# Gated delta rule on one core: keys projected first, projection and scan joined in one block, the projection's last column written among the scan's first steps

## What is computed

```python
h = rms_norm(x) ;  q, k, v = silu(short_conv(h @ w_in))      # width-5 convolution along time
k, q = l2_norm(k), l2_norm(q) ;  g, beta = decays from h @ w_in
# chunks; L strictly lower, decay = exp(cum_i - cum_j)
T = (I + tril(k_beta @ k.T * decay, -1))^-1
state loop: v_new = u - w @ state ; o = (q e^g) @ state + (q k.T * decay) @ v_new ; state = ...
out = o_forward + flip(o_backward)
```

## Time and profile before

| what | value |
|---|---|
| median of 3 runs | 3502.65 us (3502.46 to 3506.62) |
| the profiled execution, its own time | 3501.62 us |
| span of the profiled execution | 3499.8 us |
| PE busy share of the span | 88% |
| DVE, ACT, POOL busy share | 59%, 39%, 33% |

### The profile page before, as it was taken

The page is one execution under the profiler, slowest core; times in us unless marked ns, Lnnn a source line. Parts: engine busy times, 40 slices in busy tenths (PEclk is TensorE's granted clock), DMA queues, the critical chain, the costliest instruction groups (busy, mean ns, idle before and its releaser), DMA issues. The chain is left out here.

```text
span 3499.8 us, 44483 instructions
## 1 busy us (share of the span) xinstructions
PE 3083.2 (88%) x16273; PEld 2512.1 (72%) x16273; DVE 2072.1 (59%) x3903; ACT 1377.9 (39%) x2733; POOL 1141.7 (33%) x1254
## 2 busy tenths in 40 slices
PE   5899988978998877889999999868878688899888
PEld 3578855746787656678878877768867688688777
DVE  6689975566997747767761015457755587101333
ACT  1366465124663641336652203444323443221222
POOL 1236421321562214421014332334423344424330
PEclk9999999989999999999999999979989799899999
DMA  6323322621233244300002122023131232513421
GB/s 209 120 78 93 106 95 82 208 96 46 79 97 130 85 133 154 106 24 1 1 29 84 50 97 87 26 77 84 48 108 31 77 83 49 163 49 108 141 88 43
DMA packets 227147, 303.15 MB, mean 87 GB/s; under 512 B 40911, under 2 KB 142031, under 8 KB 224753
## 3 DMA queue, kind: packets, MB, share of 16 engines
q1 hardware_dynamic: 215410, 279.33, 26.0%
q10 hardware_dynamic: 11520, 20.98, 1.6%
HBM read 241.91 MB, written 58.33 MB: 86 GB/s over the span
## 5 line engine op out<-in xcount | busy, mean ns | idle before, releaser
L815 PE MATMUL psum<-qs,hT 128*128 128x512 f32 x1344 | 309.3, 392 | 6.0 <-POOL qs L900 6.0
L815 PEld LDWEIGHTS psum<-qs,hT 128*128 128x128 f32 x1344 | 254.0, 189 | 61.2 <-issue 5.4
L2679 PE MATMUL psum<-hTs,cws 128*128 128x512 f32 x1056 | 261.6, 409 | 16.7 <-POOL hTs L2934 14.9
L2366 PE MATMUL psum<-bhsn,bringn 128*128 128x512 f32 x1152 | 263.5, 391 | 13.9 <-POOL bringn L2422 13.0
L2366 PEld LDWEIGHTS psum<-bhsn,bringn 128*128 128x128 f32 x1152 | 217.0, 189 | 60.5 <-issue 13.4
L2679 PEld LDWEIGHTS psum<-hTs,cws 128*128 128x128 f32 x1056 | 208.0, 199 | 61.7 <-POOL hTs L2934 15.3
L2366 PE MATMUL psum<-bhsa,bringa 128*128 128x512 f32 x1056 | 241.7, 391 | 2.9 <-POOL bringa L2422 2.9
L2366 PEld LDWEIGHTS psum<-bhsa,bringa 128*128 128x128 f32 x1056 | 199.4, 189 | 44.8 <-issue 3.3
L1595 PE MATMUL psum<-w_out,oys 128*128 128x512 f32 x768 | 180.5, 397 | 30.6 <-DVE w_out L1678 28.6
L1595 PEld LDWEIGHTS psum<-w_out,oys 128*128 128x128 f32 x768 | 146.7, 192 | 64.4 <-DVE w_out L1678 29.5
L980 DVE TENSOR_SCALAR_CACHE_REDUCE junk<-score,cand 128x384 uint8<-128x384 f32 x248 | 186.8, 810 | 2.2
(11 more groups left out here) (514 smaller groups left out, 7053.8 us busy)
## 6 DMA issues: line engine op xcount, KB each, us to landing
stg<-in_w_in SPq DMA_DIRECT2D x96, 256.0 KB, 2.7
score<-in_w_ada SPq DMA_DIRECT2D x32, 512.0 KB, 3.8
pj<-ptmp ACTq DMA_DIRECT2D x64, 256.0 KB, 2.1
dlb<-blocks SPq DMA_DIRECT2D x32, 512.0 KB
dlb<-in_w_in SPq DMA_DIRECT2D x22, 512.0 KB, 4.0
wa<-in_w_ada SPq DMA_DIRECT2D x8, 1024.0 KB, 8.3
oyf<-yTd SPq DMA_DIRECT2D x16, 512.0 KB, 6.3
ostg<-in_w_out SPq DMA_DIRECT2D x16, 512.0 KB, 5.7
```

The lines of the kernel that those rows point to most:

```text
L815: mm = pe.matmul(bank(m), lhs, rhs, start=(kc == 0 and x == 0), stop=(kc == KC - 1 and x == 2))
L2366: mm = pe.matmul(ps[:, m, :], lhs[:, fs], h, start=(kc == 0 and x == 0), stop=(kc == KC - 1 and x == 2))
L2679: mm = pe.matmul(ps[:, u % 4, :], w, h, start=(kc == 0 and x == 0), stop=(kc == KC - 1 and x == 2))
```

## The change

- Columns are now keys (0 to 3), queries (4 to 7), values (8 to 11), through a table `KIND`. Everything tied to a column moves with it: `normalise_k` runs in iterations 2 to 5, `back` and `keep_k` in 3 to 6. Query squares use a staging place of their own.
- In group 0 the decays are loaded beside the input chunks, split before column 0 and projected on PE before column 2. Their small PSUM results move into bank 7.
- Tile pair 0 is prepared in iterations 7 to 9, and its blocks are solved by DVE inside the projection: 10 steps of `substitute` after column 9's convolution, 5 after column 10's. Of pair 1 the decays, the key Gram product, `decayed` and the stores of its blocks are also in the projection.
- Both stages share one block. The scan's loop starts at -1. The last column's convolution, SiLU, turn and copy, and the turn and copy of the column before it, are issued by the scan's code (`last.convolve`, `last.silu`, `last.turn`, `last.keep`) between its first steps. Scan tiles that lie on memory of the projection wait for its last matmul or last copy.
- The order of the engines at `now` -1 and 0 is written out separately.

```diff
-def stage_conv(k, hg, hs, d, sc, ahead):
+def stage_conv(k, hg, hs, d, sc, ahead, block):
+    KIND = (1, 0, 2)
+    def column(c):
+        return KIND[c // HG], c % HG
...
                 if kc == 3:
                     sp.dma_start(taps5[:, :, :], t["conv_w_2"][0].rearrange("c (x n) -> c x n", x=3)
                                  [:, :, hg * HG * D2:(hg + 1) * HG * D2]).then_inc(s_in, 16)
+                    if decays:
+                        prepare_decays()
-            if decays:
-                prepare_decays()
...
-            for r in range(2):
-                if r == 0:
-                    sp.wait_ge(sc.s_NLT, 1)
-                else:
-                    sp.wait_ge(sc.s_NLx, 1)
-                store_blocks(sp, t, sc, 0, r, sc.NLT[0] if r == 0 else sc.NLx)
-                load_row(sp, t, sc, hg, 1, r)
-            sp.wait_ge(s_wlo, C - BASE)
-            for r in range(2):
-                load_blocks(sp, t, sc, 0, r, sc.Lb)
+            for st in range(2):
+                for r in range(2):
+                    load_row(sp, t, sc, hg, st + 1, r)
+                sp.wait_ge(sc.s_NLT, 2 * st + 1)
+                store_blocks(sp, t, sc, st, 0, NLTs[st][0])
+                sp.wait_ge(sc.s_NLx, st + 1)
+                store_blocks(sp, t, sc, st, 1, sc.NLx)
+                if st == 0:
+                    sp.wait_ge(s_wlo, C - BASE)
+                    for r in range(2):
+                        load_blocks(sp, t, sc, 0, r, sc.Lb)
...
+            if decays:
+                project_decays()
+            for c in range(2, C):
+                project(c)
+                if decays and c == 2:
+                    turn_decays()
+                if decays and c == 4:
+                    sum_decays()
+                if decays and c == 5:
+                    turn_cum()
                 after(c - 2)
+                if 3 <= c < HG + 3:
+                    back(c - 3)
+                if c == 8:
+                    for r in range(2):
+                        gram_keys(0, r)
+                if c == 9:
+                    for r in range(2):
+                        gram_queries(r)
+                if c == 10:
+                    for r in range(2):
+                        gram_keys(1, r)
+            last.turn = after
```

On DVE, in the projection:

```diff
+            for c in range(C - 1):
+                if c == 10:
+                    for r in range(2):
+                        decayed(1, r)
                 convolve(c)
+                if decays and c == 3:
+                    soft_decays()
                 if decays and c == 4:
                     sum_decays()
...
+                if 2 <= c < HG + 2:
+                    normalise_k(c - 2)
+                if c == 8:
+                    for r in range(2):
+                        decayed(0, r)
+                if c == 9:
+                    for r in range(2):
+                        attend(r)
+                    substitute(dve, sc, sc.Lb, 0, range(0, 10))
+            substitute(dve, sc, sc.Lb, 0, range(10, 15))
+            last.convolve = convolve
```

The scan, with SP's start and then PE's additions:

```diff
-def stage_delta(k, hg, d, sc):
+def stage_delta(k, hg, d, sc, block, last):
-        TIMES = range(-3, NT + 1)
+        TIMES = range(-1, NT + 1)
...
+            sp.wait_ge(last.s_mm, 2 * (last.column + 1))
             sp.dma_start(merge[:, :, :], t["c_merge"]).then_inc(s_m, 16)
+            for r in range(2):
+                load_blocks(sp, t, sc, 1, r, Lb[1])
...
+                if now == -1:
+                    queries(0)
+                    queries(1)
+                    last.turn(last.column - 1)
...
+                if now == 0:
+                    last.turn(last.column)
```

The scan on ACT:

```diff
+                if now == -1:
+                    decay(2, 0)
+                    decay(2, 1)
+                    last.keep(last.column - 1)
+                    continue
+                if now == 0:
+                    keep_x(0, 0, 0)
+                    keep_x(0, 1, 0)
+                    weigh(2, 0)
+                    weigh(2, 1)
+                    last.silu(last.column)
+                    decay(3, 0)
+                    keep_x(0, 0, 1)
+                    keep_x(0, 1, 1)
+                    last.keep(last.column)
+                    merge_half(0, 0)
+                    merge_half(0, 1)
+                    keep_x(0, 0, 2)
+                    keep_x(0, 1, 2)
+                    merge_last(0, 0)
+                    merge_last(0, 1)
+                    decay(3, 1)
+                    weigh(3, 0)
+                    weigh(3, 1)
+                    continue
```

The scan on POOL:

```diff
                 if now == -1:
+                    pool.wait_ge(last.s_mm, 2 * (last.column + 1))
                     widen(0, 0)
                     widen(0, 1)
+                    clear(X, s_X0)
                     start_blocks(1)
+                if now == 0:
+                    clear(S, s_S0)
+                    pool.wait_ge(last.s_cv, last.column + 1)
```

The scan on DVE, and the caller:

```diff
                 if now == -1:
-                    substitute(0, range(0, 9))
+                    attend(1, 0)
+                    attend(1, 1)
+                    turn_first(0, 0)
+                    turn_first(0, 1)
+                    last.convolve(last.column)
+                    continue
+                if now == 0:
+                    merge16(0, 0)
+                    merge16(0, 1)
+                    decayed(2, 0)
+                    attend(2, 0)
+                    decayed(2, 1)
+                    attend(2, 1)
+                    solve_blocks(1, range(0, 2))
+                    merge32(0, 0)
+                    merge32(0, 1)
+                    solve_blocks(1, range(2, 15))
+                    turn_first(1, 0)
+                    turn_first(1, 1)
+                    continue
...
+                    with k.nc.Block() as block:
                         with ExitStack() as conv:
...
+                            last = stage_conv(k, hg, hs, d, sc, conv_ahead if hg == 0 else None, block)
                         with ExitStack() as scan:
...
+                            stage_delta(k, hg, d, sc, block, last)
```

More of the change, by code:

```diff
@@ L2509, in __init__ @@
         self.Rb = [self.rows[:, r].rearrange("p (h q) -> p h q", h=HG) for r in range(2)]
+        self.NLT1 = [self.rows[:, 2].rearrange("p (h q) -> p h q", h=HG),
+                     k.sb(ctx, f"dnlt1_{hg}", [P, HG, P], side="right")[:, :, :]]
+        self.Tc = k.sb(ctx, f"dtc_{hg}", [P, 2, HG, 16], side="right")
+        self.part = k.sb(ctx, f"dpart_{hg}", [P, 2, HG, 15], side="right")
+        self.subs = 0
+        self.s_ti, self.s_sub, self.s_solved = (k.sem(n) for n in ("Tc_init", "subst", "solved"))
         (self.s_relu, self.s_dk, self.s_md, self.s_nbd, self.s_G, self.s_QK, self.s_NLT, self.s_NLx,
@@ L2606, in stage_conv @@
         s_hlo = [k.sem("hT_lo_even"), k.sem("hT_lo_odd")]
-        block = ctx.enter_context(nc.Block())
+        NLTs = (sc.NLT, sc.NLT1)
+        KEYS_IN = ((4, 5), (6, 7))
+        QUERIES_IN = (6, 5)
+        last = Store()
         @block.sync
@@ L2907, in _ @@
                     turned(c - 2)
-                if HG + 3 <= c < 2 * HG + 3:
-                    keep_k(c - HG - 3)
-                if c == 8:
+                if 3 <= c < HG + 3:
+                    keep_k(c - 3)
+                if c in (7, 9):
                     for r in range(2):
-                        make_decay(act, sc, d.cum[:, r, 0 if r == 0 else NT - 1, hg * HG:(hg + 1) * HG], 0, r)
-                if c == 9:
+                        decay((c - 7) // 2, r)
+                if c in (8, 9):
                     for r in range(2):
-                        weigh(r)
+                        weigh(c - 8, r)
+            last.silu, last.keep = silu, turned
         @block.gpsimd
@@ L3177, in _ @@
                         load_ec(now, r)
-                if ahead(now + 2):
+                if now >= 0 and ahead(now + 2):
                     sp.wait_ge(s_NLT, 2 * (now + 2) + 1)
@@ L3203, in gram @@
                 u = 2 * st + r
-                if u:
+                if u == 4:
+                    pe.wait_ge(last.s_raw, 2 * (last.column + 1))
+                else:
                     pe.wait_ge(s_NLT, u)
@@ L3212, in gram, with queries @@
                     mm = pe.matmul(gbank(1)[:, h, :], d.kT[:, h, tk(st, r)], d.qT[:, h, tk(st, r)], start=True, stop=True)
+                mm.then_inc(s_QK, 1)
+            def queries(r):
+                pe.wait_ge(s_NLT, 2 + r + 1)
+                for h in range(HG):
+                    mm = pe.matmul(bank(6 + r)[:, h, :], d.kT[:, h, tk(1, r)], d.qT[:, h, tk(1, r)], start=True, stop=True)
                 mm.then_inc(s_QK, 1)
@@ L3303, in _ @@
             for now in TIMES[:-1]:
-                prep, inv, scan = ahead(now + 2), on(now), on(now - 1)
+                prep, inv, scan = now >= 0 and ahead(now + 2), on(now), on(now - 1)
+                if now == -1:
+                    queries(0)
+                    queries(1)
+                    last.turn(last.column - 1)
                 if inv:
```

(8 more changed lines are left out.)

328 lines of the change are left out of this document (165 added, 163 removed).

## The result

| what | before | after |
|---|---|---|
| median of 4 runs | 3502.56 us (3501.12 to 3506.62) | 3471.47 us (3468.96 to 3476.09) |
| ratio | | 0.9922, 95% interval 0.9903 to 0.9941 |
| the profiled execution, its own time | 3501.62 us | 3468.96 us |
| span of the profiled execution | 3499.8 us | 3467.1 us |

The account below looks back on a forecast made before the run. PE was busy 88% of the span, but only latency bounded the seam between projection and scan. Seam gains 21.1 + 20.9 minus projection costs 7.4 and 8.4 gave 26.2 us: 3476 us, bounds 3466 to 3486, chance 0.60.

Parts of the forecast that it names:

- the turn: Seam from last projection matmul to pair 1 turned for step 1: 38.5 us forecast, gaining 21.1 and 20.9 us.
- PE after P8: PE's work from the end of column 8's matmuls to the last projection matmul: 42.8 us.
- E at about 2298: Sign of a right forecast: group 0's last projection matmul ends at about 2298 us in the trace.
- DVE and SP: Chain from column 8's convolution through block stores, load and solve; last convolution ends 18.5 us after the last projection matmul.
- rival C: At the seam, blocks land early and PE sets the pace: 17 us more gained, 3459 us; chance 0.15.
- Step 0: Seam work from the last convolution's end to the turned pair 1: 20.0 us.
- The Squares' 2.1 us: Projection cost: query Squares, 1.1 us each, stand ahead of `keep_k` in two iterations, +2.1 us per group.
- +0 there: Projection, group 0's first key: no added stall, as decays are projected in between; group 1 was given +3.5 us.
- the Gram products: Projection cost: key products of pair 1 come earlier in PE's order, +1.8 us per group.
- A, DVE's key chain: In iterations 2 to 5 DVE falls behind and key columns lose time; 3510 us at 4.3 a column; chance 0.06.
- B, late blocks: Pair 0's or 1's blocks come 8 us late, all of it showing at the seam: 3492 us; chance 0.17.
- D: Something else bounds step 1; the seam keeps its 59 us and only costs remain: 3518 us; chance 0.02.

Follow-up runs that it names:

- second comparison: Both kernels run once more, unaltered: 3499.49 us for the kernel before, 3470.65 us for the changed kernel, ratio 0.9934.
- a5: Changed kernel, with SP holding the stores of pair 0's blocks until half of column 10 is projected: 3497.14 us, ratio 0.9997 to the kernel before.
- a3: Changed kernel, with the two stages again in separate blocks so all engines meet between them: 3480.31 us, ratio 0.9945 to the kernel before.
- a6_split_back: Changed kernel, with the second half of a key's turn back placed between the next column's halves on PE: 3449.42 us, ratio 0.9861 to the kernel before.
- a1_early_load: Changed kernel, with side 0's block load issued between the fourth and fifth store of side 1: 3474.34 us, ratio 0.9938 to the kernel before.

## Why the prediction was right, and where its terms were off

**The sum.** Over both profiles of each kernel:

| us | before | after | measured | forecast |
|---|---|---|---|---|
| projection, group 0 | 189.9, 192.8 | 193.2, 192.7 | +1.6 | +7.4 |
| projection, group 1 | 174.1, 173.5 | 179.7, 182.3 | +7.2 | +8.4 |
| the turn, group 0 | 59.6, 60.2 | 40.9, 41.8 | -18.6 | -21.1 |
| the turn, group 1 | 59.4, 60.0 | 40.4, 40.2 | -19.4 | -20.9 |

The sum is -29.2, forecast -26.2. That the sum is this close is partly luck, since two errors stood against each other: the cost in group 0 was 5.8 us too high, the gain at the two seams 4.0 too high. Followed to the last output addition of the scan, the gain from E is 20.5 us in group 0 (244.0 to 223.5, each the mean of two profiles) but 16.2 in group 1 (241.0 to 224.8). Of the 3.2 us that group 1 gives back there, 0.9 are in step 1; the later steps have the rest, since both profiles of the changed kernel have two steps of 27.8 us in that group and the kernel before has none and one. That makes 27.9 in all, beside the 28.8 between medians of the second comparison. The agreement holds chance too: group 0's projection began 4.2 us sooner on the mean, and the stretch behind the scan, which the change does not touch, took 527.4 and 526.8 us before and 529.0 to 530.5 in all twelve profiles of changed kernels. The forecast had no term for these 2 to 3 us, and their cause was not sought.

**PE after P8.** P8 is 2240.9, from the first profile. E came at P8 + 42.5, forecast 42.8; in group 1 also 42.5. The sign "E at about 2298" did not show: E is 2283.4, since that projection began 10.2 us sooner by chance and took 3.3 us more than before instead of 7.4. The first product with the state, 2352.2 before and 2326.7 after, is 25.5 us earlier, or 15.3 without those 10.2, where some 14 were forecast.

**DVE and SP.** Convolution 8 was done at P8 + 10.1, not 11.3: the 1.2 us that I added for POOL was not there, since the split had ended when it began. First stores at P8 + 10.9 (12.0), both sides stored at 21.8 (22.1, the first side taking 5.76 for 5.1), blocks at P8 + 34.2 (34.7), wait 8.2 (9). The last convolution ended at E + 18.7 and E + 18.0, forecast 18.5. That the wait is on the path is what a5 shows; that DVE and not PE is the late one, which separates the forecast from rival C, follows from a5 and a3 together.

**Step 0** took 22.2 and 22.4 us from there, not 20.0: this is the term mis-sized at the seam. The forecast allowed 0.6 us for pair 2's second key product, 2.0 us of waiting at the 32 merge and 0.4 for semaphores. The timeline shows 1.57 us behind that product, then 1.74 and 0.52 at the merge, and one 0.18 us solve operation stretched to 1.17 beside a masking on POOL: 1.0, 0.3 and 1.0 of the 2.2 us.

**Costs in the projection.** The start of group 0 was given 2.5 us; PE waited 0.86 us for the split weights. The Squares' 2.1 us can be what shows in group 0, where the last two stalls of the turn back are 5.07 and 3.40 for 4.09 and 1.72, but in group 1 they are 3.75 and 1.98, no more than before. In group 0 the first key's two stalls, 2.95 and 2.64, fell to 2.13 and 0.75 with the decay work in between, which the forecast ("+0 there") left out. In group 1 the first key's stall was forecast at 6.3 us; it is 6.15 in one profile and 3.30 in the other, where column 2 ran slower; column and stall together are 17.3 us in the one and 16.1 in the other. One term was too small in both groups: the Gram products. The forecast added 1.8 us for pair 1's, but half of pair 0's had also stood behind E. In the windows view of each projection PE does 18 of these matmuls before, 2.3 us, and 48 after, 6.0 us. So group 1's +7.2 for 8.4 is right in size with its terms shifted: in the first profiles PE is idle 14.3 us for 13.9, and busy 165.3 for 160.2.

**The rivals.** A, DVE's key chain: no PE wait in the key columns is above 5.07 us except the first key's 6.15, which the forecast had, and most convolutions beside a split are slow in the opening operation alone (1.9 for 0.75); that 6.15 is made by one whose taps were slow too (7.26 for 5.25). B, late blocks: the mechanism is real (a5), but nothing delayed them. C, PE sets the seam: the blocks were not early enough to show it, and of the two runs meant to make them so one gained nothing, the other 1.6 and 0.5 us at the turn. D: the seam lost 19 us. Settled steps are unchanged, 26.2 us between turns in both kernels, with some of 27.8 in every profile of either. The windows view tells the two kinds apart. These are two steps in a row of the changed kernel's group 0:

```profile
2350.99:2377.15 26.16, 22.51 (x209) 21.25 (x208) 21.96 (x53) 12.50 (x38) 12.32 (x12) 1.00 0.31 84
2377.15:2404.90 27.75, 24.09 (x208) 22.84 (x208) 21.98 (x52) 12.49 (x38) 12.32 (x12) 0.94 0.29 79
```

DVE, ACT and POOL work as long in both; PE does the same matmuls in 24.09 us instead of 22.51, at a granted clock of 0.94 instead of 1.00. The twin profiles' turns differ with the clock too: 40.9 us at 0.85 and 41.8 at 0.78 in group 0.

**Rule against trace.** The port rule of the Trainium skill ("SBUF — State Buffer", section "Who interferes with whom") would have given 5.2 us for my 2.2 beside convolution 8 and the last one. Measured: 0 at the one and 1.8 at the other (7.84 for 6.05). For the last convolution alone, where the rule says 2.6 and I said 1.0, the truth lies between.

## What to carry to other kernels

Before moving work under another stage, list what each engine has queued from the moved step's last input to the stage's end: the one with the longest queue pays for a late transfer in full, though it is idle at that moment and another engine looks busy. Put independent work that is ready ahead of such a wait, and never a store that is waited for behind a large load in one queue. In a6_split_back every us of PE's idle time that went was worth 1.4 us in group 0 and 2.1 in group 1, since with it the columns ran at a higher granted clock. And before a wait is put down to a step, say between which two events of the trace the step lies: the wait for the ec row lay outside the 30 us that it was to explain, and cost nothing.

## What the runs showed of the hardware

- Of four 4 KB stores issued right behind a 512 KB load in the same queue, the last two landed 5.2 us after their issue (a1_early_load); eight with no load ahead of them landed in 1.8 us (the DMA view's medians).
- Loads of the blocks, 1 MB in all, landed 11.0 us after their issue alone and 12.3 us with 512 KB of rows behind them.
- Four taps of a convolution and two maskings, 5.25 and 2.50 us apart, took 7.03 and 4.55 us together.
- With group 0's stalls of the turn back gone (0.75 to 5.07 us each), the same matmuls of a projection took 172.2 us instead of 176.6, the granted clock being 0.97 for 0.94.
- Of the scan's settled steps, none to two in a group take 27.8 us instead of 26.2, mostly those from the turned pair 3 to 4 and 4 to 5. They are those with a granted clock of 0.94 for 1.00, in every profile kept. Why the clock falls in one step and not in its neighbour stays open.
